# Laying the slots of attention and HGRN evenly over the dense chunks of a hybrid decoder step

## What is computed

```
h = rms_norm(x, norm_mix) * (1 + sc_a) + sh_a          # adaLN, modulation = silu(c) @ w_ada + b_ada
q, k, v, rq, rf, ri, rg, ga, gr = split(h @ w_in)
o_attn = window-128 GQA with sinks and ALiBi (16 q heads, 4 kv heads)
o_rec  = HGRN2(silu(rq), 1 - sigmoid(rf), ri, log forget gate)     # 8 heads, 128 x 128 state each
o_rec  = rms_norm(o_rec, hgrn_norm) * silu(rg)
x = x + g_a * ((sigmoid(ga) * o_attn + sigmoid(gr) * o_rec) @ w_out)
x = x + g_m * (relu(h2 @ w_up)^2 @ w_down)             # h2: second adaLN norm
y = rms_norm(x, final_norm)
```

## The kernel before

| list | begins | used up at | chunks without a slot after it |
|---|---|---|---|
| prep | q 0 | q 0, first tile | 41 chunks, to rq 0 |
| attention | rq 0 | ri 1, third tile | 5 |
| pairs 0 and 1 | ga 0 | rq 2, first tile | 14 |
| pair 2 | rf 3 | ri 3, third tile | 4 |
| pair 3 | gr 0 | gr 1, second tile | 42 to the first chunk of out |

## Time and profile before

### The profile page before, as it was taken

The page is one execution under the profiler, slowest core; times in us unless marked ns, Lnnn a source line. Parts: engine busy times, 40 slices in busy tenths (PEclk is TensorE's granted clock), DMA queues, the critical chain, the costliest instruction groups (busy, mean ns, idle before and its releaser), DMA issues.

```text
span 1275.0 us, 22074 instructions
## 1 busy us (share of the span) xinstructions
PE 1182.6 (93%) x8733; PEld 1115.2 (87%) x8733; DVE 728.5 (57%) x1549; ACT 535.4 (42%) x993; POOL 182.7 (14%) x144
## 2 busy tenths in 40 slices
PE   5799999988998998988989999979999999999996
PEld 4699977877888887988978999869999999999996
DVE  5733466646476677387576555464644636546464
ACT  3423346666554454564544323344232232322324
POOL 1400000000132223033221001042010110110100
PEclk9899989989999998999998999979999999999998
DMA  9777412021322230302221228302223223222202
GB/s 309 210 188 267 159 34 67 34 67 34 111 80 69 69 99 4 109 29 91 78 68 53 79 87 273 95 6 81 86 69 98 81 85 100 67 77 89 67 34 75
DMA packets 121258, 120.45 MB, mean 94 GB/s; under 512 B 19268, under 2 KB 111132, under 8 KB 120869
## 3 DMA queue, kind: packets, MB, share of 16 engines
q1 hardware_dynamic: 121157, 119.06, 29.6%
HBM read 109.22 MB, written 11.80 MB: 95 GB/s over the span
## 4 chain that ended last, share of the span: by engine, by line
PE 50%; DVE 11%; ACT 2%; issue 1%; POOL 0%; DVEq 0%; ACTq 0%; POOLq 0%
PE PS L767 43%; PE PS L726 2%; DVE wR L1302 1%; DVE qt L1460 1%; DVE att L1478 1%; PE PS L882 1%; DVE kt L1461 1%; PE PS L928 1%; PE PS L935 1%; DVE xhat L1270 1%; PE PS L925 1%; DVE S L1510 0%; DVE b L1367 0%; DVE S L1501 0%; DVE tmp L1286 0%
## 5 line engine op out<-in xcount | busy, mean ns | idle before, releaser
L767 PE MATMUL PS<-hR,wR 128*128 128x288 f32 x3744 | 538.1, 302 | 1.9 <-ACT tmp L1072 1.0
L767 PEld LDWEIGHTS PS<-hR,wR 128*128 128x128 f32 x3744 | 514.0, 192 | 11.6 <-issue 6.4
L767 PE MATMUL PS<-actR,wR 128*128 128x288 f32 x1920 | 258.6, 295 | 1.8 <-DVE actR L1444 1.8
L767 PEld LDWEIGHTS PS<-actR,wR 128*128 128x128 f32 x1920 | 255.4, 188 | 2.9 <-DVE actR L1444 2.0
L1302 DVE TENSOR_TENSOR wR<-raw,wR 128x512 fp32r<-128x512 f32 x256 | 202.8, 792 | 86.9 <-ACT wR L997 79.8
L997 ACT ACTIVATE wR<-raw 128x512 fp32r<-128x512 f32 x256 | 161.8, 632 | 140.6 <-PE PS L767 132.9
L1607 POOL TENSOR_TENSOR D<-b 128x512 f32<-128x512 f32 (+1 forms) x56 | 68.3, 1219 | 508.2 <-PE PS L855 285.3
L1634 POOL TENSOR_TENSOR actR<-tmp,actR 128x576 fp32r<-128x576 f32 x32 | 46.2, 1445 | 304.8 <-DVE actR L1355 304.8
L1355 DVE CAST actR<-tmp 128x576 fp32r<-128x576 f32 x32 | 15.2, 476 | 129.5 <-ACT tmp L1091 129.5
L726 PE MATMUL PS<-wR,hR 128*128 128x256 f32 x600 | 80.7, 291 | 1.1 <-ACT rv L1065 0.5
L882 PE MATMUL PS<-qt,kt 128*128 128x64 f32 x448 | 60.3, 279 | 22.2 <-DVE qt L1460 19.0
(11 more groups left out here) (212 smaller groups left out, 1284.7 us busy)
## 6 DMA issues: line engine op xcount, KB each, us to landing
raw<-in_w_in SPq DMA_DIRECT2D x26, 1024.0 KB, 5.3
raw<-in_w_up SPq DMA_DIRECT2D x16, 1024.0 KB, 5.6
raw<-in_w_down SPq DMA_DIRECT2D x16, 1024.0 KB, 5.0
mid<-in_w_ada SPq DMA_DIRECT2D x12, 1024.0 KB, 5.3
ada<-in_w_ada SPq DMA_DIRECT2D x8, 1024.0 KB, 12.0
raw<-in_w_in SPq DMA_DIRECT2D x16, 256.0 KB, 6.0
S<-in_state_hgrn SPq DMA_DIRECT2D x8, 512.0 KB, 4.2
out_hgrn_sample<-S SPq DMA_DIRECT2D x8, 512.0 KB, 5.9
```

The costliest lines, as they stand in the source:

```text
L767: mm = pe.matmul(PS[:, 2 * x.pair + h, 0:HALF], weights(x, w, k, col), rhs[r], start=(k == 0 and n == 0), stop=(k == last and n == 2))
```

## The change

Each list of slots is given a first and a last tile, and its n slots are laid over all m chunks between them: slot number i goes to chunk number i*m//n. The plan is made ahead of the walk and each chunk takes what the plan has for it, which may be nothing. No event is added, removed or changed inside a slot, and their order stays.

| list | slots | chunks before | chunks after | where |
|---|---|---|---|---|
| prep | 4 | 4 | 9 | q 0 |
| attention | 44 | 44 | 49 | rq 0 to the ada tile ahead of ga 0 |
| pair 0 | 22 | 22 | 32 | ga 0 to 3 |
| pair 1 | 22 | 22 | 26 | rf 2, rq 2, ri 2 |
| pair 2 | 22 | 22 | 42 | rf 3, rq 3, ri 3, gr 0, rg 0 |
| pair 3 | 22 | 22 | 32 | gr 1, rg 1, gr 2, rg 2 |

```diff
--- before.py
+++ after.py
@@ -212,20 +212,19 @@
     for x in TILES:
         first.setdefault((x.kind, x.i), x.t)
 
-    work = [[prep_slots(), first["q", 0], first["rq", 0]],
-            [attention_slots(), first["rq", 0], first["ga", 1]],
-            [hgrn_slots(0), first["ga", 0], first["rf", 2]],
-            [hgrn_slots(1), first["ga", 0], first["rf", 3]],
-            [hgrn_slots(2), first["rf", 3], first["gr", 0]],
-            [hgrn_slots(3), first["gr", 0], first["gr", 2]]]
-
-    def slot(t):
-        while work and work[0][1] <= t:
-            ev = next(work[0][0], None)
-            if ev is not None:
-                return ev
-            work.pop(0)
-        return []
+    def spread(slots, begin, end):
+
+        slots, chunks = list(slots), [(x.t, c) for x in TILES[begin:end] for c in range(CHUNKS.get(x.kind, 4))]
+        for n, ev in enumerate(slots):
+            plan.setdefault(chunks[n * len(chunks) // len(slots)], []).extend(ev)
+
+    plan = {}
+    spread(prep_slots(), first["q", 0], first["q", 1])
+    spread(attention_slots(), first["rq", 0], first["ga", 0])
+    spread(hgrn_slots(0), first["ga", 0], first["rf", 2])
+    spread(hgrn_slots(1), first["rf", 2], first["rf", 3])
+    spread(hgrn_slots(2), first["rf", 3], first["gr", 1])
+    spread(hgrn_slots(3), first["gr", 1], first["gr", 3])
 
     yield ("front",)
     k_tile = TILES[first["k", 0]]
@@ -257,9 +256,6 @@
     scanning = None
     turning = None
     for x in TILES[FRONT:]:
-        while work and work[0][2] <= x.t:
-            for ev in work.pop(0)[0]:
-                yield from ev
         joint = (x.kind, x.i) in JOINT
         if pending and joint:
             yield ("ada_sum", pending)
@@ -301,7 +297,7 @@
                 yield ("lo", x.split + 1, at)
                 if at == 3 and SPLITS[x.split + 1] in AFTER:
                     yield ("load", AFTER[SPLITS[x.split + 1]])
-            yield from slot(x.t)
+            yield from plan.get((x.t, c), [])
         if turning is not None:
             yield ("y_turn", turning)
         if x.kind == "ada":
```

## The result

The changed kernel takes 1261.06 us as the median of four runs (1258.3 to 1264.86), the kernel before beside it 1278.0 us: a ratio of 0.9869 [0.9841, 0.9898], or 17 us less. The forecast was 1254.6 with a range of 1236 to 1270. The profiled execution took 1262.03 us (span 1260.3) at a mean clock of 0.963, the same as before. Measured again beside the experiments it gave 1257.09 us against 1277.07 (0.9841 [0.9822, 0.986]). So the direction and the range held; the sum came out 2.5 to 6.5 us too good, and its terms were wrong by more than that.

A forecast was written before the change was run, and what follows sets the result against it. TensorE was taken as the bound, with its waits and low clock winnable. Waits 17.2, clock 5.1 and attention 2, less tables 0.5, gave 23.8 us off the profiled 1276.8: 1253.0, or 1254.6 us as a median, range 1236 to 1270.

The forecast's parts named there:

- PE sets the end, and what it waits for in the heads can be had back by spacing: Whole kernel: TensorE, busy 93% of the span, bounds it; 29.4 us of waits in the head stretches, 17.2 to be won.
- Waits of the heads, 17.2 us: Head stretches: empty chunks let DVE catch up, so waits fall from 29.4 to 12.2 us; bounds 10 and 29.4.
- a catch-up of 1.0 us for each empty chunk: Heads: each chunk without a slot lets DVE work off 0.8 to 1.1 us of backlog, taken as 1.0.
- Head 2 takes over what head 3 had, 4.3: Head 2, moved beside rf 2 and rq 2: waits 4.3 us, head 3's 5.3 less 1 for one empty chunk.
- Clock, 5.1 us: Heads: three of five low-clock spells behind waits go, 1.7 us each; five behind output slots stay; bounds 0 and 17.
- Attention, 2 us: Attention: 44 slots over 49 chunks win 2 of 27.5 us lost to waits and clock; bounds -2 and 8.
- The end of attention, hidden: The `win` slot moves four chunks later; its later stores are covered by some 4 us, so cost 0.
- The price if uncovered: End of attention: without cover for the later window stores, up to 6 us of POOL standing.
- Tables, 0.5 us: ACT in heads 0, 2 and 6: one more Ln table load each before the norm, costing 0.5 us together; bounds 0 and 3.
- only the waits return (1260): Rival: waits are won but the clock stays low as long, without the 5.1 us: 1259.7 us; chance 0.10.
- the rival in which the backlog moves: Rival: heads 2, 3, 6 and 7 lose 3 us, no spell goes, 9.6 us remain: 1269 us; chance 0.13.
- The low clock didn't spread: Rival over 359 to 740 us: thinner mixture lowers the mean clock, slower below 0.905; at 0.87, 1292 us; chance 0.08.

The follow-up runs named there:

- each part alone: Only prep and attention, only pairs 0 and 1, or only pairs 2 and 3 laid evenly, against the kernel before: 1275.33, 1275.6 and 1272.1 us.
- the spacing with free chunks: Changed kernel with pairs 0 and 1, and 2 and 3, as joint lists, three chunks behind the scans' start in rq 2 and rq 3 without slots: 1249.57 us.

## Why the prediction was right, and where it wasn't

**PE sets the end, and what it waits for in the heads can be had back by spacing.** Right in part: net 15.5 us in all, 8.0 of them waits of the heads in the profile. Heads 0 and 5 have next to none left (the forecast had 4 and 5), head 2 has the most, the stretches behind the heads are as before (82.24 of 84 us busy at 1.00), as forecast.

**Waits of the heads, 17.2 us.** Measured 8.0. The step that failed is the reading of the earlier trace rows as a backlog, with a catch-up of 1.0 us for each empty chunk. A catch-up fits the mask, the state, `kh` and the waits without a named cause, 9.9 us before and 2.4 after (the forecast had no term of their own for them), and not the operand, 19.0 before and 17.3 after. That stands at fixed places in DVE's queue: behind the chain of an rf tile (4.63 and 2.70 us) and behind clusters of DVE's work (2.32, 1.53, 1.75, 1.02 and 2.36). Heads 1 and 4, with four and seven empty chunks, were given 0.3 and 0.2 us; they have 2.6 and 2.7. In head 1 no empty chunk lies between the cluster and the operand. In head 4 one does (24 matmuls from 548.11 us, beside the scans), and against a chain of 8.9 us, from the load at 544.79 to the operand's end, it isn't enough. Three free chunks right there took one such wait from 3.56 to 0.77. The earlier trace rows show DVE and PE alone. On ACT, ahead of those same scans in the kernel before, table loads of 1.28 us begin at 488.40 and 490.37 us, around the sigmoid that the scans need. The step left that side out, and so took a queue that stands for another engine for one that is overloaded. The load itself hardly fell, either: DVE was busy for 0.715 of the head stretches before and for 0.691 after, and in heads 0, 5 and 6 its share didn't fall at all (0.70, 0.62 and 0.74 before; 0.70, 0.70 and 0.79 after), where the prediction had it falling in every head.

**Head 2 takes over what head 3 had, 4.3.** Nearly: 5.7. One empty chunk and the same chain.

**Clock, 5.1 us.** In the head stretches of the profile 2.3, over its whole span 0.6, by the medians of the group 3.9. But each part alone loses 2.4 more than the kernel before, though it has fewer waits. The count of three spells that would go with three waits is sound only for the longest waits; the others come and go with no change of a wait. The range should have carried 4 to 5 us to both sides for that alone; it did so for another reason.

The Trainium skill (TensorE: Matmul & The Clock Gate, HAM oscillation) speaks of long gaps; that short waits cost only themselves is the prediction's own conclusion from it. Here single waits of 2.25 and 3.05 us had a low spell behind them in three profiles out of three, and output slots had one with no wait ahead, so the trace doesn't bear that conclusion out.

**Attention, 2 us.** 4.6 in the profile, of it some 1.9 clock; net 3.4 when it is done alone, though only 1.7 in the median, which the interval can't tell from nothing. It was under-sized, within its bounds.

**The end of attention, hidden.** Right: no wait of PE came of it, and SP's wait is over at 359.53 us, ahead of POOL's `qh` at 367.25. The price if uncovered was wrong, though: the 7.5 us shrank to 1.05 instead of moving along.

**Tables, 0.5 us.** 0.7 us in three waits on L1019, the longest 0.3. Right in size. The prediction counted one load more for each of three heads; there are seven: three at the tanh (L1080), three at the norm (L1018) and one at an exponential (L1134).

**The rivals.** None came about as a whole. That only the waits return (1260) is nearest in time, by chance: less of the waits, more of attention, and some of the clock. (The 1269 us of the rival in which the backlog moves leave out the terms of attention and tables; with them it is 1267.) The low clock didn't spread: the mean in the heads is 0.96, not under 0.905.

## What to carry to other kernels

Before spacing work out, follow each long wait back over the last ten microseconds through all engines: if the engine that it names was simply busy, free time helps, where it lies right ahead of the wait; if it was idle in between, waiting for another engine ahead of work that PE doesn't need yet, it is a chain, and here moving it or making it shorter helped. Ask as well whether what PE waits for needs that chain at all, or only stands behind it in the queue. Even spacing is a good first step that costs nothing, and taking a table load out of each chain, with chunks left free behind it, brought another 12 to 16 us (1244.8 against 1257 to 1261 us), 7.6 of them in net time. Where a clock falls in spells, compare kernels by span times clock as well as by time, and don't read a change of less than some 5 us in the time of one of them as the change's own.

## What was unexpected

Low spells come behind small-matmul slots with no wait ahead, at the same instruction in one kernel and not in another with equal waits: 24 matmuls in 4.60 or 3.11 us. Between runs of one kernel this is worth up to 9 us of 1250.

DVE's operand takes 0.43 us at 407.96 and 1.32 us at 409.36 in the changed kernel, and 1.51 at 674.25 in the spacing with free chunks. Both long ones ran beside a product on POOL, the first of them this one:

```profile
408.98 1.41 POOL L1623 TENSOR_TENSOR qh<-qs,eb 128x576 f32<-128x576 f32 x1 [0.91 <-DVE kt L1457]
409.36 1.32 DVE L1456 TENSOR_TENSOR qt<-qs,D 128x256 f32<-128x256 f32 x1
```

That the two hinder each other is read from the overlap alone; no run here took POOL's product away.
